# Prompt attention on two heads per step behind the key blocks, and the late modulation blocks inside gated heads one and two

## The reference, cut to what matters

```python
mod = silu(c) @ w_ada + b_ada                         # (1 + 8 rows) x 6 * 1024: three pairs of shift, scale, gate
shift1, scale1, gate1, shift2, scale2, gate2 = split(mod)
h = rms_norm(x, norm1_g) * (1 + scale1) + shift1
q_a, k_a, v_a, q_g, k_g, v_g, og_g, gk_lr, gate_a, gate_b = split(h @ w_in)
o_a = attention(q_a, k_a, v_a)       # 8 heads of 64; prompt: causal 512 x 512 with a position bias
                                     # sample: 2048 cached positions (16 pages) + 4 new ones, best 3 blocks of 256
o_g, s_new = gated_linear_attention(q_g, k_g, v_g, gk_lr, state)   # 4 heads, keys of 128, values of 256
merged = sigmoid(gate_a) * (o_a @ w_branch_a) + sigmoid(gate_b) * (o_g @ w_branch_b)
x = x + gate1 * (merged @ w_out)
h2 = rms_norm(x, norm2_g) * (1 + scale2) + shift2
x = x + gate2 * mixture_of_experts(h2)                # 32 experts, 2 per token
```

## Time and profile before

| | us |
|---|---|
| median of 3 runs | 1411.27 |
| lowest and highest of them | 1405.19, 1416.59 |
| the profiled execution, as timed | 1408.55 |
| its span, first to last instruction | 1406.8 |

### The profile page before, as it was taken

One profiled execution on the slowest core, in us unless ns is written; L12 is line 12 of the kernel. 1 busy time (PEld: TensorE's weight loads), 2 busy tenths in 40 slices (PEclk: granted clock), 3 DMA queues, 4 the chain that ended last, 5 costly groups with the idle time before them and its releaser, 6 DMA issues.

```text
span 1406.8 us, 17946 instructions
## 1 busy us (share of the span) xinstructions
PE 1259.7 (90%) x6825; PEld 707.1 (50%) x6825; DVE 396.4 (28%) x835; ACT 237.7 (17%) x529; POOL 190.2 (14%) x282
## 2 busy tenths in 40 slices
PE   4999968999999999999999999899788878887886
PEld 2345422446776768688888745534233323332432
DVE  3489832643233332400000034511100110010104
ACT  3122211423232322210000022100000000000002
POOL 2324213310011111210000000111010110000000
PEclk9999977989999999999999999799999999999998
DMA  9969999969242423342200824699999999999975
GB/s 357 340 241 330 341 417 390 386 216 292 61 157 53 117 53 116 82 114 53 95 25 1 348 71 113 235 403 426 422 425 425 423 424 423 426 424 420 425 329 194
DMA packets 116153, 372.60 MB, mean 265 GB/s; under 512 B 10948, under 2 KB 56533, under 8 KB 96622
## 3 DMA queue, kind: packets, MB, share of 16 engines
q1 hardware_dynamic: 93664, 308.96, 57.0%
q0 software_dynamic: 19280, 55.49, 11.7%
q10 hardware_dynamic: 3134, 7.16, 1.5%
HBM read 359.29 MB, written 22.36 MB: 271 GB/s over the span
## 4 chain that ended last, share of the span: by engine, by line
PE 64%; DMA 26%; DVE 4%; SPq 3%; issue 2%; ACT 1%; POOLq 0%; ACTq 0%; DVEq 0%
PE ps L1645 61%; DMA ring<-in_w_exp_up 19%; PE ps L1656 3%; SPq L442 2%; DMA work<-in_x_prompt 2%; DMA ring<-in_w_ada 2%; DMA ring<-in_cache_k 1%; DMA ring<-in_cache_v 1%; SPq L440 1%; DVE work L1339 1%; DVE work L1634 0%; SPq L466 0%; DVE work L1639 0%; DVE ring L1137 0%; ACT hx L687 0%
## 5 line engine op out<-in xcount | busy, mean ns | idle before, releaser
L1645 PE MATMUL ps<-ring,work 128*64 128x512 f32 (+2 forms) x1856 | 449.4, 640 | 85.3 <-DMA ring<-in_w_exp_up 49.2
L1645 PEld LDWEIGHTS ps<-ring,work 128*64 128x64 f32 (+2 forms) x1856 | 153.4, 145 | 347.2 <-issue 271.5
L1645 PE MATMUL ps<-ring,hx 128*32 128x256 f32 (+3 forms) x1392 | 251.4, 421 | 6.7 <-ACT hx L710 3.6
L1645 PEld LDWEIGHTS ps<-ring,hx 128*128 128x128 f32 (+1 forms) x1392 | 152.7, 151 | 90.7 <-issue 66.3
L1645 PE MATMUL ps<-hx,ring 128*128 128x272 f32 x768 | 179.1, 393 | 0.6 <-DVE work L1339 0.6
L1645 PEld LDWEIGHTS ps<-hx,ring 128*128 128x128 f32 x768 | 145.2, 190 | 31.2 <-DVE work L1339 1.1
L1645 PE MATMUL ps<-work 128*32 128x256 f32 (+10 forms) x850 | 110.3, 362 | 12.2 <-DVE work L1075 6.3
L1645 PE MATMUL ps<-work,ring 128*128 128x272 f32 (+2 forms) x464 | 97.7, 369 | 0.7 <-ACT ring L964 0.7
L1599 DVE TENSOR_TENSOR work<-work,ps 128x256 f32<-128x256 f32 x32 | 13.5, 421 | 279.1 <-ACT work L1002 279.1
L1645 PEld LDWEIGHTS ps<-work,ring 128*128 128x128 f32 (+1 forms) x464 | 81.4, 188 | 18.6 <-issue 2.7
L1002 ACT ACTIVATE work<-ps 128x256 f32<-128x256 f32 x32 | 12.3, 383 | 433.7 <-PE ps L1645 433.7
(11 more groups left out here) (297 smaller groups left out, 810.3 us busy)
## 6 DMA issues: line engine op xcount, KB each, us to landing
ring<-in_w_exp_down SPq DMA_DIRECT2D x32, 2048.0 KB, 22.5
ring<-in_w_exp_gate SPq DMA_DIRECT2D x31, 2048.0 KB, 17.8
ring<-in_w_exp_up SPq DMA_DIRECT2D x31, 2048.0 KB, 22.2
ring<-in_w_ada SPq DMA_DIRECT2D x12, 2048.0 KB, 20.1
ring<-in_cache_k SPq DMA_DIRECT2D x64, 256.0 KB, 8.3
ring<-in_cache_k POOLq DMA_DIRECT2D x64, 256.0 KB, 6.4
ring<-in_cache_v SPq DMA_DIRECT2D x64, 256.0 KB, 14.0
ring<-in_cache_v POOLq DMA_DIRECT2D x64, 256.0 KB, 6.1
```

The lines of the kernel that those rows point to most:

```text
L1645: return pe.matmul(out, lhsT, rhs, start=start, stop=stop, **k)
```

## The change

- The prompt loop takes two heads per step: 16 units (`UNITS`) of a pair of heads and one tile of queries. Scores of both heads are two matmuls on different row halves of PE into two banks; bias, maximum and reciprocal are one DVE instruction for both; exponential and division stay one per head; the transposes of both heads go to banks 6 and 7 (before: two banks in turn, one per unit), copied by one ACT instruction; the products of both heads stand side by side in bank 1 (before: two banks in turn), copied by one DVE instruction.
- The loop starts behind the key blocks: `scores(0)` stands ahead of the last key fold, and there is no wait on the modulation any more. Each step z from 1 to 16 has one value block. The second half's sample weights are turned in steps 2 to 6 (`later_weights_turned`), into memory of their own.
- Modulation blocks 4 to 7 come after the blocks of gated head one in the stream, 8 to 11 after those of head two. PE multiplies four of them in each head, right behind `kend_tr`, in bank 6 (`LATE_BANK`); `late_mod_turned` follows the head's `sample_parts`. The transposes of the late rows and their four small stores move into head three, the first two loads that read them to the end of head four.
- `cT` is kept in a copy for it. `SLOT_ORDER` follows the new order. SP waits for `late_out` ahead of the third expert's loads.

```diff
-        ADA += [modulation_block(i) for i in range(FIRST_ADA, 12)]
         for i in range(DEC_B * PAGES // 8):
             PAGED[("v", i)] = add_block(("v", i), PAGES // 4, (s("pv_s"), i + 1))
...
             GLA.append((a, b))
+            if h < 2:
+                ADA += [modulation_block(i) for i in range(4 * h + 4, 4 * h + 8)]
...
                 if n == AFTER_SPARE:
-                    sp.wait_ge(s("p_tr"), 32)
+                    sp.wait_ge(s("p_pv"), 2 * PAIRS * PT // 2)
...
+                    if far:
+                        dve.tensor_tensor(sc_p[:, z % 3, :, 0:far], ps[:, banks, 0:far], bc(rbfar[:, heads].unsqueeze(2), [P, 2, far]), ALU.add)
+                    link(dve.tensor_tensor(sc_p[:, z % 3, :, far:n], ps[:, banks, far:n], near[:, heads, 2 * P - (n - far):2 * P], ALU.add))
+                    dve.tensor_reduce(st[:, c:c + 2], sc_p[:, z % 3, :, 0:n], AX.X, ALU.max, negate=True).then_inc(s("sc_max"), 1)
+                if z == 0:
+                    softmax_max(1)
+                if z == 1:
+                    softmax_norm(1)
...
+            pe.wait_ge(s("qk_T"), NORMED)
+            scores(0)
             keys_folded(3)
...
-            for i in range(FIRST_ADA, 12):
-                ada(i)
-            mod_turned(7)
-            mod_turned(11)
-            page_values(0)
-            pe.wait_ge(s("mod_set"), 2)
-            for x in range(32 + 3):
...
+            weights_turned()
             pe.wait_ge(s("v_ready"), 5)
+            pe.wait_ge(s("sc_taken"), 8)
+            for z in range(1, UNITS + 3):
+                if z < UNITS:
+                    scores(z)
+                if TURN_AT <= z <= TURN_AT + 4:
+                    later_weights_turned(z - TURN_AT)
+                if z == SELECT_AT:
+                    selected(0)
+                if z <= PAGES:
+                    page_values(z - 1)
+                if 2 <= z <= UNITS + 1:
+                    y = z - 2
+                    if y:
+                        pe.wait_ge(s("p_T"), y)
+                    for o in range(2):
+                        pe.wait_ge(s("p_norm"), 2 * y + o + 1)
+                        for j in range(y % PT + 1):
+                            last = turn(ps[:, 6 + o, P * j:P * j + P], sc_p[:, y % 3, o, P * j:P * j + P])
                     last.then_inc(s("p_tr"), 1)
+                if z >= 3:
+                    y = z - 3
+                    p, i = y // PT, y % PT
                     pe.wait_ge(s("p_T"), y + 1)
+                    if y:
+                        pe.wait_ge(s("p_ov"), y)
...
                     for j in range(i + 1):
+                        for o in range(2):
+                            h = 2 * p + o
+                            last = mm(ps[64 * o:64 * o + 64, 1, 0:P], v_tok[:, j, AD * h:AD * h + AD],
+                                      pt_p[:, y % 2, o, P * j:P * j + P], j == 0, j == i, skip_group_check=True)
                     last.then_inc(s("p_pv"), 1)
...
                 last.then_inc(s("kend_tr"), 1)
+                if h < 2:
+                    for i in range(4 * h + 4, 4 * h + 8):
+                        late_ada(i)
+                elif h == 2:
+                    late_rows_turned()
                 landed(pe, b_blk)
                 pe.wait_ge(s("vg_ready"), 5 * h + 5)
                 sample_parts(0, 0, wo).then_inc(s("part_ps"), 1)
+                if h < 2:
+                    late_mod_turned(h)
...
+                    if i == 0 and h < 3:
+                        pe.wait_ge(*(after("mod_middle") if h == 0 else (s("mod_set"), 2) if h == 1 else after("late_rows")))
```

More of the change, by code:

```diff
@@ L806, in _ @@
             act.dma_start(v_sample[0].rearrange("b t h d -> (b t) (h d)"), v_tok[0:NS, PT, :]).then_inc(s("v_out"), 16)
[L807 to L823, removed]
+            act.activation(cT_kept, cT.rearrange("p k c -> p (k c)"), ACT.Copy).then_inc(*done("cT_kept"))
+            weights()
+            for z in range(UNITS + 2):
+                if TURN_AT <= z <= TURN_AT + 4:
+                    later_weights(z - TURN_AT)
+                if z == SELECT_AT:
+                    sample_heads(0)
+                if z < UNITS:
+                    n = P * (z % PT + 1)
+                    c = 32 + 8 * (z % 2)
+                    act.wait_ge(s("sc_max"), z + 1)
+                    for o in range(2):
+                        act.activation(sc_p[:, z % 3, o, 0:n], sc_p[:, z % 3, o, 0:n], ACT.Exp, bias=st[:, c + o:c + o + 1],
+                                       accum_out=st[:, c + 2 + o:c + 3 + o]).then_inc(s("sc_exp"), 1)
+                if z == 0:
+                    act.wait_ge(*after("cT_kept"))
+                    exponent(1)
+                if z >= 2:
+                    y = z - 2
+                    n = P * (y % PT + 1)
                     act.wait_ge(s("p_tr"), y + 1)
@@ L826, in _ @@
                         act.wait_ge(s("p_pv"), y - 1)
[L827 to L831, removed]
+                    act.activation(pt_p[:, y % 2, :, 0:n], ps[:, 6:8, 0:n], ACT.Copy).then_inc(s("p_T"), 1)
             sample_heads(1)
@@ L836, in _, with late_mod_taken, late_rows_sent @@
             act.activation(halves(gkT), wide(2), ACT.Identity, bias=const("bias_row")[:, 0:1]).then_inc(*done("gk_ready"))
[L837 to L841, removed]
+            def late_mod_taken(g):
+                act.wait_ge(w_used, 4 * g + 8)
+                act.activation(late_mod_rows[g], ps[:, LATE_BANK, :], ACT.Copy).then_inc(s("last_mod_rows"), 1)
+            def late_rows_sent():
+                act.wait_ge(*after("late_ps"))
+                act.activation(late_rows, grid(ps[0:KD * (DEC_B + 1), LATE_BANK, :], 4), ACT.Copy).then_inc(*done("late_rows"))
+                act.wait_ge(*after("late_rows"))
+                for a in range(4):
+                    act.dma_start(mod_dram[a].rearrange("c (k p) -> k c p", p=P), late_rows[:, a, :]).then_inc(s("late_out"), 16)
             def late_source(a, first, *dims):
@@ L1092, in _ @@
                 hat_taken(k)
-            for i in range(FIRST_ADA):
-                mod_taken(i)
+            mod_taken()
             dve.wait_ge(s("mod_tr"), 1)
-            mod_set(0, 16, 0)
+            mod_set(0)
             def sample_modulated(a, ready):
@@ L1901, in _ @@
                     for j in range(i + 1):
-                        last = mm(ps[rows, (7, 1)[y % 2], 0:P], v_tok[:, j, AD * h:AD * h + AD], pt_p[:, y % 2, P * j:P * j + P],
-                                  j == 0, j == i, skip_group_check=True)
+                        for o in range(2):
+                            h = 2 * p + o
+                            last = mm(ps[64 * o:64 * o + 64, 1, 0:P], v_tok[:, j, AD * h:AD * h + AD],
+                                      pt_p[:, y % 2, o, P * j:P * j + P], j == 0, j == i, skip_group_check=True)
```

272 lines of the change are left out of this document (151 added, 121 removed).

## The result

| | us |
|---|---|
| before, median of 4 runs on the same chip | 1410.23 (1405.19 to 1416.59) |
| after, median of 4 runs | 1370.3 (1368.87 to 1372.72) |
| ratio, with its 95% interval | 0.972 (0.969 to 0.975) |
| after, the profiled execution: timed, span | 1372.72, 1371.0 |

The account below looks back on a forecast made before the run. Loads bound 161 to 270 us, PE the later gated heads. Span 1406.8 - 64.5 (earlier first gated product) + 17.5 (heads) = 1359.8 us, 1361.5 as timed; forecast set at 1363 us, range 1350 to 1379.

Parts of the forecast that it names:

- The two limits: Before the change, loads limit 161 to 270 us; later, in the gated heads, PE is the limit and loads have room.
- Loads at 386 GB/s: From 161.4 us, the remaining loads arrive at 386 GB/s, taking 95.3 us; last value block at 256.7, 260 with the hole.
- The rivals of 330 and 406 GB/s: Load stage: 330 GB/s gives 1379 us, chance 10 in 100; 406 without hole or lag gives 1353, chance 8.
- Bytes: Loads still to come after 161.4 us: 36.8 MB, with one key block, 2.1 MB, as the key rest.
- The step that failed: Second softmax starts at about 184 us as before, so its division is done at about 197.5.
- The hole: Loads pause near 202 us, as the seventh block's issue waits for block 1 behind the softmax: 3 us (0 to 6).
- The pace of a step: Prompt loop: PE needs 4.2 us per step with a pair's heads side by side, 5.5 without overlap.
- The rival of the single banks: Prompt loop: single banks chain PE, DVE and ACT, 9.8 us per step, 1443 us; chance 3 in 100.
- The clock: Prompt loop: PE falls to the low clock; half the steps gives 1387 us, chance 8 in 100; all gives 1417, chance 3.
- The tail: End of the prompt loop: 10.5 us from the last value block to the first gated product, 6.91 before.
- The heads: Gated heads: late modulation products, turned rows, transposes and additions add 17.5 us (15.5 to 24).
- the 1417 us: Prompt loop: by the skill's rule the clock falls in every step, so no change in time; chance 3 in 100.

Follow-up runs that it names:

- the move alone: Kernel before with its old single-head loop, but modulation blocks moved into gated heads one and two: 1399.47 us, ratio 0.9909.
- the base: The changed kernel run again without edits, beside the follow-up kernels on its chip: 1371.36 us, ratio 0.9705.
- both edits: Changed kernel with POOL's value pages held until all key blocks are transposed and the second half's weights turned in steps 4 to 8: 1364.57 us, ratio 0.9661.
- only the pairs: Changed kernel with its pair loop, but modulation blocks 4 to 11 again ahead of the value blocks and their products ahead of the loop: 1388.98 us, ratio 0.9838.

## Why the prediction was right, and where it was off

*The two limits* were read rightly, and the two partial kernels show it from both sides: with the faster loop alone the loads set the pace, with the move alone PE does.

*Loads at 386 GB/s* held from 220 to 260 us (383 to 390 in the windows), but not at the start: from 161.4 to 170 us, while the last key pages came, it was 281 GB/s, which costs 2.3 us. Why so little comes at a full DMA share there stays open. The rivals of 330 and 406 GB/s for the whole stage did not come.

*Bytes* was a mis-sized term. SP's queue reaches its 50.47 MB at 268.10 us in after:

```profile
161.40:268.10 106.70, 85.48 (x806) 39.72 (x800) 62.70 (x111) 37.65 (x97) 34.81 (x64) 0.92 0.99 355
161.40:170.00 8.60, 8.00 (x54) 3.78 (x47) 5.79 (x3) 0.77 (x2) 3.59 (x6) 1.00 1.04 281
```

That is 37.9 MB, 1.1 more than predicted, 2.8 us at 386 GB/s. I had taken one key block for the rest at 161.4 us from PE's last product alone. The bytes of the queues in the trace of before would have told me better: 2.7 MB, within my bounds of half a block to two.

*The step that failed* is "184.3 + 9.05 + 2.2 + 1.3 and some hand-overs, about 197.5". It took over the start of the second softmax from the trace of before, as if the key blocks ahead of it were not touched by the change. But POOL's value pages moved forward as well, from 197.84 to 163.03, past SP's last key pages. The softmax came 8.2 us later and the turned weights at 205.10 instead of 197.5; the rest of that sum held (192.25 + 9.05 + 2.2 + 1.3 = 204.8). I had named POOL's queue nowhere in that step, though each queue that a load is moved past counts.

*The hole* was put in the right place with the right cause, but at 3 us (0 to 6). Against 386 GB/s, 200 to 220 us miss (386 - 276) x 10 + (386 - 250) x 10 kB = 2.46 MB, 6.4 us. Turning the weights two steps later fills most of it even with late keys. Holding POOL back, so that the softmax starts where the prediction had it, leaves 2.5 us, near the 3 predicted; so the size of the hole was off mainly because the softmax was late.

*The pace of a step* was 4.2 us predicted and 4.5 to 4.6 measured over the eight steps to 246.38, which hold more than the sum had: the turned sample weights in the first four, `selected(0)` in the others. Pairs overlap. The rival of the single banks is out: it wanted 9.8 us per step, and PE is busy 17.9 and 18.1 us of these 18.1 and 18.5.

*The clock* rival is out as well: in every window of after from 210 to 280 us the mean is 1.00, and in the base the lowest of them is 0.88. After the 6.02 us wait one value block took 3.35 us, and the next 1.92, so the low level lasted for less than the 15 us that I allowed. The last value block starts 9.7 us after the predicted 262. The last value bytes come 8.1 us after the predicted 260: 2.8 for bytes, 3.4 for the hole (6.4 against 3) and 2.3 for the slow start make 8.5, and 0.4 is left over. PE starts the block 3.65 us behind them, where I had allowed for 2 of lag.

*The tail* was 10.5 predicted, 11.18 measured.

*The heads* were right: 17.5 predicted, 17.8 measured (9.4, 7.8, 0.7, 0). The four blocks had landed: no load is waited for behind `kend_tr`. DMA delivers 29 GB/s from 300 to 310 us, when the first head's blocks were there.

*In sum*: the first gated product 10.4 us late, heads 0.3 over, the rest 0.5: 1359.8 + 11.2 = 1371.0 in span. The median of after is 0.7 below that span where I had allowed for 3.2 above mine, so 7.3 us remain between forecast and median. The mechanism was right and three terms of the load stage were too small or missing: the bytes, the hole and the rate of the first 8.6 us. All three erred to the same side. The 3.9 us by which the median lay lower against the span than I had allowed went the other way; that is luck.

## What to carry to other kernels

Where a stage that waits for bytes stands next to one that waits for PE, moving bytes from the first to the second pays until the first stage's compute sets its pace: here 13.3 us with the old loop, which then was the limit, and 16.4 on top of the faster one. When a load is moved forward, follow each queue that issues it: a second queue's pages overtake what the first still has under way, and the data on the path comes late although the total rate is the same. Count the bytes still under way at the start of a stage from what each queue has been given and has moved, and keep enough work that needs nothing late (here two more value blocks) ahead of a wait: with both, the kernel runs at 1364.57 us, 6.8 us below the change as it stands, and most of that comes from either one (1366.95 and 1368.09).

## What the runs showed of the hardware

**Two queues share the rate, and the older load pays.** POOL's first value page is issued at 163.03, some 4 us behind SP's last key page. The view of the queues from 170 to 180 us gives packets, MB and share of the DMA engines' time, for after (q0 is POOL's, q1 SP's) and, behind the dots, for the kernel with both edits, where q0 shows one packet:

```profile
q0 software_dynamic: 744, 2.45, 65.1%
q1 hardware_dynamic: 740, 1.35, 37.4%
...
q1 hardware_dynamic: 2064, 3.75, 103.6%
```

With POOL's pages beside them, SP's key pages get 135 GB/s instead of 375, and SP's queue is through with them at 176.8 us; in the kernel with both edits it is 171.4, in the kernel before 169.9. The two queues do not get half each: they move the same number of packets, but POOL's data packets here are of 4096 bytes and SP's of 2048. The chain of waits of after shows the link to the last key block:

```profile
158.87 21.58 DMA ring<-in_cache_k
```

The chain of the kernel with both edits shows the link to the last key block but one; the last was there when DVE came to it:

```profile
154.87 15.89 DMA ring<-in_cache_k
```

In after DVE could take the last key block only at 180.47. The rate from 170 to 180 us is 383 GB/s in the one and 378 in the other, so nothing was lost but the order. The Trainium skill says in "DMA: Bandwidth & Descriptors", section "Queues, rings and completion order", that each DMA engine takes packets from its queues in turn; the trace agrees, with 744 and 740 packets in 10 us.

**A wait of some 3 us cost the clock little.** From 250 to 260 us of after PE is busy 5.96 of 10 us, waits 3.33 us for a load and stays at a mean of 1.00; the value block behind that wait takes 1.92 us. In the changed kernel's other execution it waits 3.50 us there and the block takes 2.50. In the kernel with both edits the block behind a wait of 2.57 us takes 3.38, and with only the pairs it is the same (2.58, then 3.38). The block after it takes 1.92 again in each. So such a wait costs up to 3.38 - 1.92 = 1.5 us on one block, and sometimes nothing. The Trainium skill, "TensorE: Matmul & The Clock Gate", section "HAM oscillation — how this bites in real kernels", describes a loop whose work per step is shorter than its wait for the next load, and in which every step falls back to the low clock. In the prompt loop, with over 4 us of work per step, only single blocks did so. The modulation products of the kernel with only the pairs agree with the section: behind waits of 2.35, 2.98, 3.94 and 3.74 us for `in_w_ada` four blocks in a row took 3.62, 3.42, 3.47 and 3.27 us. So the 1417 us that the prediction drew from that section is not what it says of this loop, whose expected waits of 1.2 us were shorter than its work.
